# Decode attention: the layout and the issue point of the forget-bias rows

## The reference, cut to what matters

```python
past_suffix = flip(cumsum(flip(past_lf, axis=1), axis=1), axis=1) - past_lf   # per sequence, position, head
bias_k = concatenate([past_suffix, -g_new], axis=1)
s = einsum('bqhd,bshd->bhqs', q, k_all) * ATTN_SCALE
s = s + bias_q[:, :, :, None] + bias_k[:, :, None, :]      # the same bias for all 8 queries of a head
p = softmax(where(causal, s, NEG_INF)); o = einsum('bhqs,bshd->bqhd', p, v_all)
```

## Time and profile before

| | us |
|---|---|
| median of 3 runs | 2484.23 |
| lowest, highest | 2477.99, 2488.96 |
| the profiled execution | 2484.29 |
| its span, first to last instruction | 2482.7 |
| PE busy in it | 2348.4 |
| mean granted TensorE clock | 0.973 |

### The profile page before, as it was taken

How to read it: one execution, slowest core, us unless ns; L and a number is a source line. 1 busy time by engine, 2 the same in 40 slices (tenths; PEclk the granted TensorE clock), 3 DMA queues, 4 the chain that set the end, 5 groups by cost and what they waited for, 6 DMA issues and landing times.

```text
span 2482.7 us, 45242 instructions
## 1 busy us (share of the span) xinstructions
PE 2348.4 (95%) x18252; PEld 2140.8 (86%) x18252; DVE 1065.7 (43%) x1433; ACT 812.7 (33%) x982; POOL 468.8 (19%) x877
## 2 busy tenths in 40 slices
PE   7999999997889999999989996999999999999997
PEld 6999999996666666666659995999999999999997
DVE  6443443433333333333326436444444444444445
ACT  3233333332333333333312334333333332333334
POOL 2110000101333333333311232111111111111221
PEclk8999999998999999999989997999999999999998
DMA  8554343545899999999976654676676766688883
GB/s 251 158 168 148 113 148 128 183 132 169 288 339 346 342 313 346 351 339 309 339 255 208 193 160 135 228 238 238 227 248 219 250 230 235 226 282 267 286 301 101
DMA packets 340126, 585.85 MB, mean 236 GB/s; under 512 B 20624, under 2 KB 283092, under 8 KB 336304
## 3 DMA queue, kind: packets, MB, share of 16 engines
q0 software_dynamic: 70752, 309.02, 35.2%
q1 hardware_dynamic: 269232, 274.86, 34.8%
HBM read 564.06 MB, written 109.39 MB: 271 GB/s over the span
## 4 chain that ended last, share of the span: by engine, by line
PE 79%; DMA 11%; issue 4%; DVE 3%; ACT 2%; POOL 1%; POOLq 0%; SPq 0%; DVEq 0%; ACTq 0%
PE ps L815 14%; PE ps L817 14%; PE ps L816 14%; DMA kraw<-in_cache_fox_k 6%; PE ps L853 6%; PE ps L855 6%; PE ps L854 6%; PE ps L1042 3%; PE ps L1047 2%; DMA kraw<-in_cache_win_k 2%; PE ps L1067 2%; PE ps L1127 1%; PE ps L1031 1%; PE ps L1033 1%; PE ps L1032 1%
## 5 line engine op out<-in xcount | busy, mean ns | idle before, releaser
L1626 DVE TENSOR_TENSOR w_lo<-raw,w_hi 128x2048 fp32r<-128x2048 f32 (+2 forms) x250 | 525.5, 2102 | 791.7 <-ACT w_hi L1295 785.4
L1295 ACT ACTIVATE w_hi<-raw 128x2048 fp32r<-128x2048 f32 (+2 forms) x250 | 439.2, 1757 | 1054.0 <-PE ps L817 741.5
L815 PE MATMUL ps<-act_hi,w_hi 128*128 128x320 f32 x1616 | 500.7, 310 | 5.7 <-DVE gs L2059 5.7
L817 PE MATMUL ps<-act_hi,w_lo 128*128 128x320 f32 x1616 | 500.5, 310 | 0.0
L816 PE MATMUL ps<-act_lo,w_hi 128*128 128x320 f32 x1616 | 500.5, 310 | 0.0
L853 PE MATMUL ps<-act_hi,w_hi 128*128 128x320 f32 x1040 | 327.6, 315 | 0.0
L855 PE MATMUL ps<-act_hi,w_lo 128*128 128x320 f32 x1040 | 321.4, 309 | 0.0
L854 PE MATMUL ps<-act_lo,w_hi 128*128 128x320 f32 x1040 | 321.3, 309 | 0.0
L815 PEld LDWEIGHTS ps<-act_hi,w_hi 128*128 128x128 f32 x1616 | 304.4, 188 | 5.9 <-issue 5.9
L816 PEld LDWEIGHTS ps<-act_lo,w_hi 128*128 128x128 f32 x1616 | 304.4, 188 | 0.0
L817 PEld LDWEIGHTS ps<-act_hi,w_lo 128*128 128x128 f32 x1616 | 304.3, 188 | 0.0
(11 more groups left out here) (374 smaller groups left out, 3753.6 us busy)
## 6 DMA issues: line engine op xcount, KB each, us to landing
raw<-in_w_gate_up SPq DMA_DIRECT2D x88, 1024.0 KB, 6.3
kraw<-in_cache_fox_k POOLq DMA_DIRECT2D x128, 512.0 KB, 6.9
vraw<-in_cache_fox_v POOLq DMA_DIRECT2D x128, 512.0 KB, 7.5
raw<-in_w_in SPq DMA_DIRECT2D x60, 1024.0 KB, 7.6
raw<-in_w_gate SPq DMA_DIRECT2D x32, 1024.0 KB, 15.3
raw<-in_w_down SPq DMA_DIRECT2D x32, 1024.0 KB, 6.1
out_win_k_sample<-in_cache_win_k POOLq DMA_DIRECT2D x64, 510.0 KB, 5.8
out_win_v_sample<-in_cache_win_v POOLq DMA_DIRECT2D x64, 510.0 KB, 4.2
```

The costliest lines, as they stand in the source:

```text
L815: pe.matmul(ps[:, bk_, 0:T], w_hi[:, slot, k, :], xh[:, x_k, :], start=(k == k0), stop=False)
L817: mm = pe.matmul(ps[:, bk_, 0:T], w_lo[:, slot, k, :], xh[:, x_k, :], start=False, stop=(k == k1 - 1))
L1295: act.activation(w_hi[:, slot, 0:kt, :], raw[:, pslot, 0:kt, P * slot:P * slot + P], ACT.Copy).then_inc(hi_done, 1)
L1626: dve.tensor_tensor(w_lo[:, slot, 0:kt, :], raw[:, pslot, 0:kt, P * half:P * half + P], w_hi[:, slot, 0:kt, :].bitcast(F32), ALU.subtract) ...
```

## The change

1. `scratch_fb` is laid out (head, query, sequence, position), with one copy of the bias for each of the 8 queries: 4 MB instead of 0.5 MB. It is stored by 8 DMAs, one for each query, of all 128 partitions each (512 KB), in place of 8 DMAs of 16 partitions (64 KB).
2. `load_bias` reads 16 separate rows (2 heads by 8 queries) in each of its four DMAs, in place of 2 rows read 8 times. What it writes is the same.
3. The bias of sequence b is issued in step 20 of sequence b-1, between that step's key and value block, in place of step 1 of b. The bias of sequence 0 is issued behind key block 3 in place of ahead of it.

The panels of the gate weights are as they were.

```diff
-        fbd = nc.dram_tensor("scratch_fb", (DB, HF, NPG * P), F32, kind="Internal").ap()
+        fbd = nc.dram_tensor("scratch_fb", (HF, DT, DB, PAST), F32, kind="Internal").ap()
...
-            for b in range(DB):
-                pool.dma_start(fbd[b].rearrange("h (g t) -> g h t", t=P), fbx[NPG * b:NPG * b + NPG]).then_inc(fb_st, 16)
+            for q in range(DT):
+                pool.dma_start(fbd[:, q].rearrange("h b (g t) -> (b g) h t", t=P), fbx[:]).then_inc(fb_st, 16)
...
-            pool.wait_ge(fb_st, 16 * DB)
+            pool.wait_ge(fb_st, 16 * DT)
...
-                    rows = fbd[b, 2 * j:2 * j + 2].unsqueeze(1).broadcast_to([2, DT, PAST])
+                    rows = fbd[2 * j:2 * j + 2, :, b, :].rearrange("h q n -> (h q) n")
                     pool.dma_start(fb[32 * j:32 * j + 2 * DT, :], rows).then_inc(fb_ld, 16)
...
-                        if n == 1:
-                            load_bias(kb)
+                        if kb == 0 and n == KRING:
+                            load_bias(0)
+                        if n == 20 and kb < DB - 1:
+                            load_bias(kb + 1)
...
-                    dve.wait_ge(fb_st, 16 * DB)
+                    dve.wait_ge(fb_st, 16 * DT)
```

## The result

The changed kernel takes 2462.81 us (median of 9 runs, 2454.08 to 2469.48) against 2481.57 us of the kernel before in 9 runs: ratio 0.9925, 95% interval 0.9909 to 0.9940, 18.8 us faster. The forecast was 2460 us. Its sum was nearly right and its parts were not, as the experiments show.

A forecast was written before the change was run, and what follows sets the result against it. PE was taken as the bound, in the decode stage nearly so, waiting behind the bias load. Gains of 16 (sequences 2 to 7), 5 (sequence 1) and 3 (sequence 0) made -24 us: 2484 to 2460, range 2440 to 2490.

The forecast's parts named there:

- The bound and the place of the loss: Decode stage, steps 1 to 3 of sequences 1 to 7: PE's windows 38.5 us too long from waits behind the bias load.
- Part 1, the stores: Bias stores before the decode stage: eight larger issues and 3.7 MB more cost 0, bounds 0 and +3 us.
- Part 2, separate rows: Bias load from 16 separate rows: the block behind it lands 1 us earlier than now.
- all goes well: Rival, 12%: the load takes 1.5 us and hides in steps 20 to 23, sequence 0 gives 5; 2441 us.
- Part 3, the place: Bias moved to step 20: steps 1 and 2 recover, block 21 is 2 us late; sequences 2 to 7 gain 16.3.
- my signs of being wrong: Block 21 landing over 11 us after issue, steps 1 to 3 staying long, or a projection wait for a panel.
- the stall only moves: Rival, 23%: PE waits late in the sequences instead, 31 us against 32.3 removed; -8 us, 2476.
- Sequence 0: Key block 3 now ahead of the bias, block 4 behind it: wait 7.3 shrinks to about 4, gain 3, bounds 0 and 8.
- The panels: A gate panel alone, issued after the bias, should cost steps 1 and 2 about 1 us in four sequences.
- The narrow destination: Rival, 15%: 16-partition rows hold all engines 5 to 10 us, PE waits at step 21; +25, 2509.

The follow-up runs named there:

- layout_only: The changed kernel with the bias issued in step 1 as before, keeping the new DRAM layout, stores and separate rows: 2463.28 us, ratio 0.9935.
- two_groups: Separate rows issued in step 1, but an unused ninth query row per head makes each bias DMA read a 2 by 8 pattern: 2478.86 us, ratio 0.9994.
- place_only: The kernel before with only the bias issue points moved as in the change; old DRAM layout, stores and repeated-row reads: 2482.01 us, ratio 1.0011.
- tiny_bias: The changed kernel with each bias DMA loading only the first 64 of 2048 positions: 2434.88 us, ratio 0.9815 to the kernel before.
- wide_dest: The changed kernel with the same 512 KB of bias loaded into all 128 partitions, bias left out of the result: 2436.07 us, ratio 0.9813.
- same_row: New layout, bias in step 1, each bias DMA reading one row 16 times by a stride-zero pattern of 16 by 2048: 2465.71 us, ratio 0.9935.
- rows128: The changed kernel with a DRAM copy of 128 rows a sequence, loaded by one 1 MB DMA onto 128 partitions in step 20: 2453.34 us, ratio 0.9890.
- spread: The changed kernel with the four bias DMAs issued one each in steps 20, 21, 22 and the next step 0: 2451.63 us, ratio 0.9885.

## Why the prediction came out, and where it was wrong

**The bound and the place of the loss** were right: PE's waits behind the bias load, 38.5 us by my sum, 92.9 - 57.6 = 35.3 by the floor. The assumption that each window holds the same work was wrong, and made the sum 3 us too large.

**Part 1, the stores: 0.** Right in its effect. The issues took 890 ns each in place of 546, within the bound, and the stage began at 578.2 us. One panel came late enough to hold ScalarE back by 1.6 us, so the margin to the bound of +3 was small.

**Part 2, separate rows: 1 us for each block behind.** This term was mis-sized, and it is the step that failed. I took a value near "as it is", because the destination stays narrow, and put only about 6 us of the 24 on it, 1 us in each of six sequences. With the place left alone it is worth 17.5 us (layout_only): 19.8 in steps 1 to 3 and 3.8 in sequence 0. I had set beside it the Trainium skill's rule on the number of engines and kept it out of the sum, since no row bore it out; a load at the ideal rate had 12%, in the rival where all goes well. two_groups shows what the shape is worth, 2479 against 2463 us for one and the same data, and the packets under way (8 to 10 against 13 to 15) show what it sets.

**Part 3, the place: most of the gain.** Wrong. With the old rows it loses 1.2 us (place_only), and with the new ones it gains 0.5 (2463.3 against 2462.8), neither of which shows beyond the noise. I priced 2 us for each sequence, all for block 21. The stretch of steps 19 to 23 grew by (127.5 - 106.6) / 6 = 3.5 us with the new rows and by 4.9 with the old, and mostly for other blocks. Block 21 had more lead than the 7.2 us that I gave it: in five of six sequences it went out 3.0 us after block 20 and not 4.6, since POOL had waited 1.62 us for PE between the two in any case and the bias issues fill that wait. So it was late by 1.2 us at most, though it took 9.7 to 12.9 us to land. What I had at nothing is key block 20, which I took to be safe because it is issued ahead of the bias: it landed 2.8 us later than before and gave the longest waits, 4.1, 2.3 and 1.2 us. The slack of steps 19 to 23, a DMA share of 0.86, was no help, since each block has only three buffers of lead. Of my signs of being wrong one came: block 21 took more than 11 us to land in three of the six sequences. "For the stall only moves" I gave 23%, and of the place alone it is what happened.

**Sequence 0: -3 us.** It got 2.5 us longer. Key blocks 3 and 4 did roughly as forecast, 7.3 us of wait becoming 1.2 and 5.0:

```profile
593.86 0.66 PE L1044 MATMUL ps<-ident,kraw 128*128 128x128 f32 x4 [1.15 <-DMA kraw<-in_cache_fox_k]
...
600.38 1.12 PE L1044 MATMUL ps<-ident,kraw 128*128 128x128 f32 x4 [4.99 <-DMA kraw<-in_cache_fox_k]
```

But I had said that the bias of sequence 1, issued in sequence 0, costs nothing where no value blocks are loaded. From step 17 on sequence 0 takes 22.0 us after and 17.1 before; its first 17 steps, where the 3 us were forecast, gave back 2.4 (54.4 to 52.0). The waits there are 1.8 and 2.4 us for key blocks 18 and 19, and block 19 took 9.6 us to land in place of 5.4, again a block issued ahead of the bias. With the old place and the new rows the sequence takes 67.7 us.

**The panels: 1 us in four sequences.** Nothing, as place_only and tiny_bias show with panels and no bias in these windows. The long windows of before had both, a panel and a bias.

**The narrow destination** was a rival at 15%, as a loss. As a mechanism it is real, and costs the changed kernel 27 us still (wide_dest). As a loss it didn't decide, because it was over-priced: I had all engines held for 5 to 10 us, and the packets took 3.3 us of them. Their time rose from 652 to 852 ns with the new shape which is 2.8 times the 309 ns of a wide load, where 50 to 100 GB/s against 408 meant four to eight times. The spread over more engines gained 17 us all the same. I had set the two against each other as if one had to be wrong.

So that -24 us was forecast and -18.8 measured is luck: two errors offset each other, a gain from the place that is not there and a gain from the rows nearly three times as large as I had it.

## What to carry to other kernels

Look at the outer dimension of both sides of a DMA before its bytes or its place: in this kernel 2 by 8 rows cost 17 us more than 16 rows of the same data, and 16 partitions as destination 27 us more than 128. Moving a load that holds the engines only moved the wait here, since every step around it has blocks with a short lead; make the load short first, then ask where it goes. Look at the blocks issued just ahead of such a load as well as at those behind it. A bulk store that hid at 4 MB stopped TensorE at 8 MB, so a copy that pays for a better load may have to be spread out itself.

## What the runs showed of the hardware that I had not expected

- A bias DMA of 16 rows whose source pattern is 2 by 8 slows the kernel as much with separate rows (2478.9 us) as with repeated ones (2479.4 on the same chip), and one whose pattern is 16 by 2048 with stride zero is as good (2465.7) as with separate rows (2463.3).
- At most 8 to 10 of the bias's 8 KB packets are under way at once with the 2 by 8 pattern, 13 to 15 with the pattern of 16 (layout_only, same_row).
- One such packet takes a median of 309 ns in a load onto 128 partitions (rows128), 852 ns where four loads onto 16 partitions each run at once (changed kernel), and 388 ns where these four are issued one by one (spread).
- A load can delay a block that was issued 0.5 us before it: with the new rows key block 20 took 9.0 us on average in place of 6.2 (changed kernel), and key block 1, just ahead of the bias in step 1, 9.6 in place of 7.2 (layout_only).
- The issue on GpSimd follows the pattern, too: a median of 584 ns for 2 by 8 against 490 ns for 16.
- 1 MB into 128 partitions is cheaper in this stage than 512 KB into 64, loaded 16 at a time: 607 us against 636 from first to last key block.
